# Five projection chunks of a mixer layer as rounded passes, its convolution dealt out among earlier chunks, and its merge work shared out anew

## The reference

```python
for l in range(DEPTH):                      # DEPTH = 2
    h = rmsnorm(x, norm_mix_g[l])
    z = h @ w_in[l]
    z_a, z_b, z_c, z_dz, z_dxbc, z_ddt, z_g = split_cols(z, IN_SPLITS)
    y_a = mixer_spatial_gating(z_a, ...)    # gelu, layer norm, 128x128 causal mixing
    y_b = mixer_pool(z_b, ...)              # causal means over 2, 4, 8, 16
    y_c = mixer_rwkv7(z_c, ...)             # 8 heads of 64, delta-rule state
    y_d = mixer_ssd(z_dz, z_dxbc, z_ddt, ...)   # causal conv of width 4, chunked scan
    proj = jnp.einsum('btkc,kcd->btkd', jnp.stack([y_a, y_b, y_c, y_d], axis=2), w_branch[l])
    gates = jax.nn.sigmoid(z_g).reshape(bsz, t_len, N_BRANCH, D_MODEL)
    x = x + jnp.sum(gates * proj, axis=2) @ w_out[l]
    h = rmsnorm(x, norm_ffn_g[l])
    x = x + (swiglu(h, ...) if l % 2 == 0 else moe_swiglu(h, ...))
return rmsnorm(x, norm_final_g)
```

## Time and profile before

| what | value |
|---|---|
| device time, median of 3 runs | 2045.9 us (2040.14 to 2046.44) |
| the profiled execution's own time | 2039.63 us |
| its span in the trace | 2037.8 us |
| busy in the span: PE, PEld, DVE, ACT, POOL | 99%, 81%, 74%, 58%, 3% |
| mixer of layer 0, of layer 1 in the trace | about 5 to 392 us, about 636 to 1015 us |

### The profile page before, as it was taken

One profiled execution on the slowest core, in us unless ns is written; L12 is line 12 of the kernel. 1 busy time (PEld: TensorE's weight loads), 2 busy tenths in 40 slices (PEclk: granted clock), 3 DMA queues, 4 the chain that ended last, 5 costly groups with the idle time before them and its releaser, 6 DMA issues.

```text
span 2037.8 us, 31706 instructions
## 1 busy us (share of the span) xinstructions
PE 2009.9 (99%) x12826; PEld 1658.6 (81%) x12826; DVE 1498.6 (74%) x1491; ACT 1174.1 (58%) x1067; POOL 54.2 (3%) x56
## 2 busy tenths in 40 slices
PE   8999999999999999999999999999999999999998
PEld 8888989999999988889987777777777777777775
DVE  4767565665545656754868888888888889898887
ACT  4536444433334437444557777676767777677775
POOL 0200010000000020001000000000000000000000
PEclk9999999999999999999999999999999999999999
DMA  7523224555554533222559999899989999899994
GB/s 307 183 91 120 105 104 147 181 186 183 183 187 151 186 124 124 105 84 104 184 189 368 373 353 369 329 365 368 362 339 357 366 361 367 342 355 368 361 365 192
DMA packets 70790, 503.93 MB, mean 247 GB/s; under 512 B 8320, under 2 KB 8576, under 8 KB 9984
## 3 DMA queue, kind: packets, MB, share of 16 engines
q1 hardware_dynamic: 69792, 499.03, 65.1%
q10 hardware_dynamic: 864, 2.95, 0.4%
HBM read 500.90 MB, written 1.05 MB: 246 GB/s over the span
## 4 chain that ended last, share of the span: by engine, by line
PE 58%; DVE 2%; ACT 0%; issue 0%; DVEq 0%; ACTq 0%
PE g L510 37%; PE m L510 19%; PE m L1218 1%; DVE ring_low L2143 1%; PE m L781 0%; PE m L554 0%; DVE arena L2051 0%; DVE h L2465 0%; PE g L980 0%; DVE rstd L2463 0%; DVE mg_low L2179 0%; DVE rstd L2021 0%; PE m L1211 0%; DVE arena L2165 0%; DVE h L2165 0%
## 5 line engine op out<-in xcount | busy, mean ns | idle before, releaser
L2198 DVE TENSOR_TENSOR ring_low<-ring,we_high 128x2048 fp32r<-128x2048 f32 x336 | 765.3, 2289 | 122.3 <-ACT we_high L1603 121.7
L1603 ACT ACTIVATE we_high<-ring 128x2048 fp32r<-128x2048 f32 x334 | 640.8, 1919 | 269.9 <-PE g L510 170.0
L510 PE MATMUL g<-we_high,hg_high 128*96 128x512 f32 x896 | 355.8, 397 | 0.0
L510 PE MATMUL g<-ring_low,hg_high 128*96 128x512 f32 x896 | 353.0, 394 | 0.0
L510 PE MATMUL g<-we_high,hg_low 128*96 128x512 f32 x896 | 351.9, 393 | 0.0
L510 PE MATMUL g<-h_high,ring_low 128*128 128x256 f32 x1232 | 345.1, 282 | 0.0
L510 PEld LDWEIGHTS g<-h_high,ring_low 128*128 128x128 f32 x1232 | 231.3, 189 | 0.0
L510 PE MATMUL g<-h_low,w_high 128*128 128x256 f32 x720 | 200.4, 282 | 0.0
L510 PE MATMUL g<-h_high,w_high 128*128 128x256 f32 x720 | 200.2, 281 | 0.2 <-DVE ring_low L2204 0.2
L510 PEld LDWEIGHTS g<-we_high,hg_low 128*96 128x96 f32 x896 | 144.3, 161 | 63.3
L510 PEld LDWEIGHTS g<-we_high,hg_high 128*96 128x96 f32 x896 | 144.6, 161 | 58.8
(11 more groups left out here) (327 smaller groups left out, 3160.3 us busy)
## 6 DMA issues: line engine op xcount, KB each, us to landing
ring<-stream SPq DMA_DIRECT2D x472, 1024.0 KB, 4.8
sw<-sw_in SPq DMA_DIRECT2D x1, 1088.0 KB, 11.0
sw<-sw_in ACTq DMA_DIRECT2D x1, 1088.0 KB, 8.0
x<-x_in SPq DMA_DIRECT2D x4, 256.0 KB, 4.3
out<-h ACTq DMA_DIRECT2D x4, 256.0 KB, 2.9
cc<-cc_in SPq DMA_DIRECT2D x1, 816.5 KB, 12.2
rep<-rep_in SPq DMA_DIRECT2D x1, 768.0 KB, 13.4
rep<-rep_in ACTq DMA_DIRECT2D x1, 768.0 KB, 8.0
```

The costliest lines, as they stand in the source:

```text
L510: return pe.matmul(o, a, b, start=start, stop=stop, skip_group_check=True)
L1603: A(we_high[n % 3][:, :], ring[:, slot, :], ACT.Copy).then_inc(high_ready, 1)
L2198: TT(ring_low[:, slot, :], ring[:, slot, :], we_high[n % 3][:, :], ALU.subtract).then_inc(low_ready, 1)
```

## The change

Chunks 12, 14, 15, 17 and 18 become split. Their high parts go to three regions of their own, `scan_first` for 12, `scan_even` for 14 and 18, `scan_odd` for 15 and 17; the last two lie over slots 1 to 4 of `z_w`, so the first high halves of the merge chunks now wait for chunk 17 or 18 to be used. `scan_high` on ScalarE and `scan_low` on VectorE are set between their other work. Chunks 0, 13 and 16 stay plain.

The convolution is done unit by unit behind the remainders of chunks 4 to 7, eight operations each time. `SIDE` is dealt out anew: six quarters before the products of `cw` and `ca` where there were four, one at new points `s0` and, for the second half of the tokens, `n`, one more at `z0`, and three instead of four at `mu`, `va` and `vr`. Behind each quarter's place the calls of `z_lows` move up by one half. The head sums use four column groups of TensorE, one for each tile of 128 features, in place of four matmuls added up. `over_heads` and the products `cw` and `ca` alternate between the two halves of its rows. The quarter of chunk 14 goes ahead of each `row` product. One product of branch C (`ar[..., 1, :]`) moves from VectorE to GpSimd, and TensorE waits for it before the first `s` product.

```diff
+SCAN_SPLIT = (12, 14, 15, 17, 18)
-SIDE = [("cw", 4), ("ss", 4), ("bo", 8), ("sr", 4), ("kt", 2)]
+SIDE = [("cw", 6), ("ss", 4), ("bo", 8), ("sr", 4), ("kt", 2)]
 for _c in range(2):
-    SIDE += [(f"s1{_c}", 1), (f"s2{_c}", 1), (f"s3{_c}", 1)]
+    SIDE += [(f"n{_c}", _c), (f"s0{_c}", 1), (f"s1{_c}", 1), (f"s2{_c}", 1), (f"s3{_c}", 1)]
     for _v in range(6):
-        SIDE += [(f"t{_v}{_c}", 1 + (_v == 0)), (f"z{_v}{_c}", 1 + (1 < _v < 5))]
+        SIDE += [(f"t{_v}{_c}", 1 + (_v == 0)), (f"z{_v}{_c}", 1 + (_v == 0 or 1 < _v < 5))]
-SIDE += [("mu", 4), ("va", 4), ("vr", 4)]
+SIDE += [("mu", 3), ("va", 3), ("vr", 3)]
...
             def head_sums(l, stage, src):
                 m_free(pe, l, stage)
                 for j in range(4):
-                    last = mm(mb(stage)[0:H, 0:T], by_head[:, j, :], src[:, j, :], j == 0, j == 3)
+                    last = mm(mb(stage)[32 * j:32 * j + 32, 0:T], by_head[:, :], src[:, j, :])
...
             def over_heads(l, name):
-                two_banks(l, name, lambda j: spread[:, j * P:(j + 1) * P], lambda j: rstd[0:H, :])
+                for i in range(2):
+                    m_free(pe, l, f"{name}{i}")
+                for j in (0, 2, 1, 3):
+                    rows = slice(64 * (j // 2), 64 * (j // 2) + 64)
+                    last = mm(mb(f"{name}{j // 2}")[:, (j % 2) * T:(j % 2 + 1) * T], spread[rows, (j % 2) * P:(j % 2 + 1) * P], rstd[rows, :])
...
+                    elif in_scan:
+                        pe.wait_ge(scan_low_ready, scan_chunk(l, n))
+                        low = ring_low[:, slot, :].rearrange("p (b m) -> p b m", b=BLK)
+                        high = scan_w(n).rearrange("p (b m) -> p b m", b=BLK)
...
+                    project_quarter(l, 14, i)
                     m_free(pe, l, f"row{i}")
...
-                    project_quarter(l, 14, i)
...
+                    side(f"n{c}")
...
+                    if c == 0:
+                        pe.wait_ge(S["ar_ready"], l + 1)
...
-                        if p:
-                            side(f"s{p}{c}")
+                        side(f"s{p}{c}")
...
+            def scan_high(l, n):
+                c = chunk0(l) + n
+                act.wait_ge(landed[c % RING], 16 * (c // RING + 1))
+                act.wait_ge(chunks_used, c - 3 if n in (15, 18) else c - 1 if n == 17 else chunk0(l))
+                A(scan_w(n), ring[:, c % RING, :], ACT.Copy).then_inc(scan_high_ready, 1)
...
                     half_free(act, l, m, b)
+                    if n < N_SLOTS:
+                        act.wait_ge(chunks_used, chunk0(l) + NZ - (1 if (2 * l * N_LATE + n) % N_SLOTS < 3 else 0))
                     A(half_slot(l, m, b), half_ring(ring, l, m, b), ACT.Copy).then_inc(z_high_ready, 1)
...
+                pool.wait_ge(S["e_ready"], 4 * (l + 1))
+                pool.wait_ge(S["rk_ready"], l + 1)
+                G.tensor_tensor(ar[:, :, :, 1, :], zc[:, 0:4, 1:T + 1].rearrange("p j (c t) -> p j c t", c=NCH),
+                                e_in.rearrange("p j (c t) -> p j c t", c=NCH), ALU.mult).then_inc(S["ar_ready"], 1)
...
-            def mixer_d_conv(l):
-                for i in range(4):
-                    g_done(dve, l, ("xbc", i))
+            def mixer_d_conv(l, i):
+                g_done(dve, l, ("xbc", i))
                 for k in range(4):
-                    z_low(l, 8 + k)
-                    for j in range(8):
+                    for j in (2 * i, 2 * i + 1):
...
+            def scan_low(l, n):
+                dve.wait_ge(scan_high_ready, scan_chunk(l, n))
+                slot = (chunk0(l) + n) % RING
+                TT(ring_low[:, slot, :], ring[:, slot, :], scan_w(n), ALU.subtract).then_inc(scan_low_ready, 1)
...
                 q.step(TT(w_log[:, :, :], c_sum[:, :, :], w_log[:, :, :], ALU.subtract), S["cum_ready"])
-                z_lows(l, 8)
+                z_lows(l, 9)
...
-                q.add(TT(ar[:, :, :, 1, :], rc, e_in.rearrange("p j (c t) -> p j c t", c=NCH), ALU.mult), v_seq)
-                z_lows(l, 12)
+                z_lows(l, 13)
...
                 for n in range(2, 8):
                     z_low(l, n)
+                    if n >= 4:
+                        mixer_d_conv(l, n - 4)
...
                 mixer_d_dt(l)
-                mixer_d_conv(l)
+                for n in range(8, 12):
+                    z_low(l, n)
+                scan_low(l, 12)
```

More of the change, by code:

```diff
@@ L241, in trunk @@
         z_w = part("z_w", 25192, [N_SLOTS, HALF])
+        scan_first = part("scan_first", 0, [CW])
+        scan_odd = part("scan_odd", 26216, [CW])
+        scan_even = part("scan_even", 28264, [CW])
         zc = tiles(4096, CT, T + 1)
@@ L654, in project_quarter @@
                     g_free(pe, l, unit)
-                w = chunk(chunk0(l) + n)
+                if part == 0:
+                    pe.wait_ge(scan_low_ready, scan_chunk(l, n))
+                low = ring_low[:, (chunk0(l) + n) % RING, :].rearrange("p (b m) -> p b m", b=BLK)
+                high = scan_w(n).rearrange("p (b m) -> p b m", b=BLK)
                 for k in range(4 * (part % 2), 4 * (part % 2) + 4):
-                    last = mm(gb(unit)[:, half * T:(half + 1) * T], w[:, DT * half + k, :], h[:, k, :], k == 0, k == DT - 1)
+                    last = three(gb(unit)[:, half * T:(half + 1) * T], high[:, DT * half + k, :], low[:, DT * half + k, :],
+                                 h_high[:, k, :], h_low[k // 4][:, k % 4, :], k == 0, k == DT - 1)
                 if part == 3:
@@ L1372, in mixer_d @@
                 mixer_a(l)
-                evacuate(l, Z_UNITS[12:14])
+                evacuate(l, Z_UNITS[12:13])
+                scan_high(l, 15)
+                evacuate(l, Z_UNITS[13:14])
                 filled(act, l, "bt")
@@ L1449, in mixer_c @@
                 for c in range(NCH):
-                    side(f"s1{c}", f"s3{c}")
+                    side(f"n{c}", f"s3{c}")
                     for v in range(LEVELS):
@@ L1661, in _ @@
                 for n in range(10):
+                    if n == 9:
+                        scan_high(l, 12)
                     act.wait_ge(chunks_used, chunk0(l) + n + 1)
@@ L1669, in _ @@
                 mixer_d_dt(l)
-                evacuate(l, Z_UNITS[10:12])
+                evacuate(l, Z_UNITS[10:11])
+                scan_high(l, 14)
+                evacuate(l, Z_UNITS[11:12])
                 mixer_d(l)
@@ L1855, in mixer_d @@
                 mix(l, 0)
+                scan_low(l, 15)
                 up = const("incl_up")
@@ L1913, in mixer_d @@
                         (q.add(ins, v_seq) if j < 3 else drain(f"yd{c}", ins))
+                    if c == 0:
+                        scan_low(l, 17)
                 m_done(dve, l, "yd1")
@@ L1920, in mixer_d @@
                 mixer_a_out(l)
+                scan_low(l, 18)
                 mix(l, 5)
@@ L1968, in mixer_c @@
                     m_done(dve, l, f"a{c}")
-                q.step(V.tensor_copy(spread.rearrange("p (h m) -> p h m", h=H), along(ident[0:H, 0:H], 64)), S["spread_ready"])
+                for o in range(2):
+                    q.add(V.tensor_reduce(small[:, 54 + 2 * o:56 + 2 * o], ident.rearrange("p (h q) -> p q h", q=64)[:, 32 * o:32 * o + 2, :], AX_X, ALU.add), v_seq)
+                dve.wait_ge(v_seq, q.n[id(v_seq)])
+                q.step(V.tensor_copy(spread.rearrange("p (a m) -> p a m", a=4), along(small[:, 54:58], 64)), S["spread_ready"])
                 for i in range(CT // 2):
@@ L2007, in mixer_c @@
                 filled(dve, l, "ss")
-                drain("ss", V.tensor_scalar(rstd[0:H, :], mb("ss")[0:H, 0:T], FLOOR, None, ALU.max))
-                z_lows(l, 9)
+                drain("ss", V.tensor_scalar(rstd[:, :], mb("ss")[:, 0:T], FLOOR, None, ALU.max))
+                z_lows(l, 10)
                 for j in range(4):
```

65 lines of the change are left out of this document (44 added, 21 removed).

## The result

| | before | after |
|---|---|---|
| device time, median of 6 runs each | 2043.95 us (2039.74 to 2046.44) | 2054.27 us (2051.58 to 2056.28) |
| the profiled execution's own time, and its span | 2039.63, 2037.8 us | 2055.88, 2054.0 us |
| mean granted clock of the profiled execution | 0.998 | 0.990 |

The ratio is 1.005, with a 95% interval of 1.0033 to 1.0067. The change makes the kernel 10.3 us slower. I had forecast 2031 us, so the prediction is wrong in size and in sign. In a second series the ratio was 1.0045 (1.0028 to 1.0062).

The account below looks back on a forecast made before the run. TensorE, busy 2009.9 of 2037.8 us, was taken as the bound. Layer 0's -4.75 and layer 1's -7.15 made -11.9 us, giving 2027.7 (profiled execution) or 2034.0 (median); it predicted 2031 us between them, range 2021 to 2040.

Parts of the forecast that it names:

- Less work on TensorE: Per layer, split chunks save 5.8 us; small products (head sums, `over_heads`, `cw`/`ca`) 5.1, which may not all show.
- the hole at the `row` products: TensorE's 1.0 us wait ahead of the first `row` product, filled by chunk 14's quarter: -1.0 us per layer.
- The clock has nothing to give: Granted clock read as 1.00 (2.4 GHz) in each stretch asked for, so no term was given to it.
- Chunk 8: Convolution operations ahead of layer 0's constants delay chunk 8's remainder on VectorE: +3.3 us in layer 0, 0 in layer 1.
- The chain to `bo`: Longer ScalarE and VectorE chain ahead of `bo`: net +1.6 us in layer 0, +2.5 in layer 1; wait 4.5 and 5.3.
- The term of +1.9 for the halves behind chunk 18: In layer 0's chain to `bo`, two of the first five high halves now wait for chunk 18's end: +1.9 us.
- `kt`: Stretch from `bo` to `kt`: about -0.5 and +0.5 us, 0 in all; wait ahead of `kt` still 1.5 to 2.
- 0.5 us for GpSimd's port: Between `bo` and `kt`, GpSimd's multiplication slows VectorE's `ka` beside it: +0.5 us.
- From `kt` on: -2.85: Quarters fill waits at `s`, `z0`, `n1` (-2.8, 0.8 given back); `over_heads` at `vr` saves 0.85: -2.85 us per layer.
- a wait in the levels: Sign named in advance: a TensorE wait appearing in the levels would show the forecast wrong.
- a small gain: Rival: sigmoid and y_high copies ahead of `later` cost 1.5 us in each of four halves; 2034 to 2040 us, chance 0.15.
- The rival on the slower side: New VectorE remainders not hidden, all ten costing 2.2 us each: +10 us, 2050 to 2056 us, chance 0.05.

Follow-up runs that it names:

- const_early: Changed kernel with layer 0's constants made on VectorE behind the remainder of chunk 3 instead of behind chunk 7; 2048.5 us, 1.0019 to before.
- rk_first: Changed kernel with VectorE's merge remainders counted as before (8, then 9) and the tenth made behind the release of `bo`; 2044.6 us, 1.0000 to before.
- old_deal: Changed kernel with the merge blocks dealt out, and remainders counted and placed, as before the change; 2036.8 us, 0.9967 to before.
- ar_back: old_deal_const with the product for `ar` back on VectorE instead of GpSimd; 2031.3 us, 0.9930 to before.
- split_alone: old_deal_const with the `ar` product back on VectorE and `head_sums`, `over_heads`, `cw` and `ca` as before the change; 2035.9 us, 0.9963 to before.
- all_three: Changed kernel with constants early, ScalarE's first-level copies ahead of sigmoid and y_high copies, tenth remainder behind `bo`'s release; 2033.4 us, 0.9946 to before.
- old_deal_const: old_deal with layer 0's constants made early too; 2032.4 us, 0.9947 to before.

## Why the prediction was wrong

The forecast's sum was -11.9 us for the profiled execution; the two spans differ by +16.2, which is 28.1 more.

**Less work on TensorE: right.** The terms of the first part make 2 x (5.8 + 5.1) = 21.8 us; 21.2 came, once the clock is taken out. Head sums (0.64 us), `over_heads` (1.13) and the hole at the `row` products came out as taken.

**"The clock has nothing to give": the step that failed first.** It was read from stretches of one execution in which the clock was 1.00, and taken as a fact of the kernel. It can be lost, and each wait of over 3 us that I forecast myself (3.3 ahead of chunk 8, 4.5 and 5.3 ahead of `bo`) had a price in clock that no term held. 15.6 of the 28.1 us are this: 7.5 behind those three waits, 6.4 behind waits that I had not forecast or took for harmless (first level of the second half, `kt`), and 1.7 behind the mixer of layer 1, a draw.

**Chunk 8: right, 3.3 forecast, 3.6 measured**, none in layer 1. With the clock it is 5.8 us (const_early), not 3.3.

**The chain to `bo`: right in place, a little long in size.** 4.5 and 5.3 forecast, 3.7 and 3.7 measured, 2.4 us less than forecast. rk_first shows the term that counted: the half and the remainder that the six quarters of `cw` put ahead. The term of +1.9 for the halves behind chunk 18 shows first at `cw` (old_deal: 1.68 and 2.64) and is covered there by the two extra quarters, except for 0.95 and 1.9 us ahead of `cg` that I had not named (2.9).

**`kt`: 2.08, inside "1.5 to 2", but for another reason.** I had 0.5 us for GpSimd's port; ar_back shows that `ka` gets its time back and the wait stays. What set it are the small products: 0.86 us less work at `over_heads`, 0.6 more wait, so 0.5 us less over both layers than the 0 that I had. The page of the Trainium skill that I weighed there ("SBUF — State Buffer") bore on a term that does not set the end. The page calls the shared ports an exclusive lock; that the lock is held for a whole instruction it says of VectorE's two-port modes, and of a product with two operands in SBUF only that it contends with GpSimd's reads. By my reading `ka` would end some 0.8 us later; it took 0.58 more (1.80 against 1.22), beside the last 0.7 us of GpSimd's product (185.11 to 187.29, `ka` from 186.57), which is near to it.

**"From `kt` on: -2.85": wrong.** It gave back 0.8 us in each layer for waits that stay or come. What came, in both layers: 6.5 us at the first level of the second half, 3.5 ahead of the side quarters of the first levels (VectorE's remainders), and 4.2 at z3, where two waits of 1.04 us stand in each layer and none stood before. That a wait in the levels would prove me wrong I had written myself. The end was right: at `va` and `vr`, by the timelines, the head sum takes 1.25 us less, a new wait of 1.1 takes that back, and the gain of `over_heads` stays. The 6.5 us is the case I had called "a small gain", the sigmoid and the y_high copies ahead of `later`. I found them "level within 0.3 us" because I counted ScalarE's own work. The sigmoid is of gate (4, 0) there, whose chunk now ends at `s3` instead of in the third level, and not one point earlier; it waits for GpSimd, and GpSimd for a product of VectorE that the deal had put behind the `s` masks. The rival's place was right, its price (1.5 us in each of four halves, 6 in all) was near (3.25 in two, 6.5 in all), by luck, since its cause was another, and its chance of 0.15 was too low.

Clock 15.6, first level 6.5, quarters 3.5, z3 4.2, `cg` 2.9, less 2.4 at `bo`, 0.5 at `kt` and the 1.6 given back: 28.2 of 28.1 us. So close a fit is in part luck, since smaller differences (chunk 8, waits under 0.3 us, 0.6 us of work) are left out and happen to cancel.

**The rival on the slower side named the wrong mechanism.** `scan_low` releases TensorE nowhere in the trace; the remainders of the split chunks are hidden as forecast, and split_alone is 0.37% faster than before.

**The two levels of the kernel before** (2039.6 and 2046), which I could not explain, are executions that lost less or more clock. The medians differ by 10.3 us and not by the 16.2 of the spans because the profiled execution of before was one of those that lost almost none, and the changed kernel has none like it: 0.992 is its best in 13 runs.

## What to carry over

Price a wait of the engine that bounds the kernel at its length plus the clock behind it: here the clock fell behind 23 of 25 waits of over 3 us, behind half of those of 1.6 to 3, and behind 1 in 100 of those of 0.8 to 1.6. When cover is dealt out anew, follow the producers of each piece of cover too: the gate that was moved from the third level to ahead of the first pulled ScalarE's queue behind a chain over VectorE and GpSimd, and the copies behind it, long ready, were late. Test such a deal by itself before judging what it came with: split chunks, small products and early constants made the kernel 0.5 to 0.7% faster (11 to 14 us), and the deal hid that behind a loss of 17 us, which two edits to the order of the queues undo as far as can be told (all_three against old_deal_const).

## What the runs showed of the hardware

One kernel's executions spread over 10 us (2039.2 to 2049.7) with nothing changed, and their mean granted clock goes along (0.998 to 0.991); a single profiled execution shows one draw of it. Every profiled execution, that of before too, lost about 1.5 to 8.5 us to the clock right behind the mixer of layer 1, a place that no edit here touches; I have not tried what makes the clock fall there. A lower clock can also cost little: where it falls inside work that covers another engine's chain, the wait at the end of the cover gets shorter (3.7 us to 2.1 ahead of `bo` in the changed kernel's layer 1, above). In split_alone the clock fell behind the waits of 1.68 and 2.64 us ahead of `cw` and stayed low for longer (0.83 and 0.80 over the stretches below), and no wait ahead of `bo` stands there; what that wait is in split_alone at full clock, no execution shows.

```profile
145.00:165.00 20.00, 18.32 (x112) 0.83 0.30 105
770.00:795.00 25.00, 22.36 (x126) 0.80 0.26 88
```

Beside GpSimd's two additions VectorE's remainders took 3.95 us for two, where a pair took 2.35 a moment before (changed kernel, 282.89 and 279.03 us).
